# Last expert group of a fused transformer layer: down weights of the third expert ahead of the next gate and up weights, last down product in four column pieces, last scatter by token halves

## What is computed

```
for e in range(N_EXPERTS):                       # 32
    hid = silu(ht @ w_gate[e]) * (ht @ w_up[e])  # 2048 -> 512, twice
    out = out + gates[:, e:e + 1] * (hid @ w_down[e])   # 512 -> 2048
...
x = x + g2 * out
return rmsnorm(x, final_g)
```

## Time and profile before

| | us |
|---|---|
| median of 3 runs | 1431.66 (1430.23 to 1432.35) |
| the profiled execution | 1430.98 |
| its span, first to last instruction | 1429.1 |
| TensorE busy | 1311.6 (92%) |
| VectorE busy | 681.7 (48%) |
| ScalarE busy | 158.0 (11%) |
| GpSimd busy | 62.1 (4%) |

### The profile page before, as it was taken

The page is one execution under the profiler, slowest core; times in us unless marked ns, Lnnn a source line. Parts: engine busy times, 40 slices in busy tenths (PEclk is TensorE's granted clock), DMA queues, the critical chain, the costliest instruction groups (busy, mean ns, idle before and its releaser), DMA issues.

```text
span 1429.1 us, 14957 instructions
## 1 busy us (share of the span) xinstructions
PE 1311.6 (92%) x5797; PEld 663.2 (46%) x5797; DVE 681.7 (48%) x1069; ACT 158.0 (11%) x424; POOL 62.1 (4%) x74
## 2 busy tenths in 40 slices
PE   4999999999999999999997998989899799888896
PEld 4686688577888635333332332333233233223332
DVE  5678788699987621432332331333233232232235
ACT  3300000295001302000000000000000000000002
POOL 1000000013000100000000000000000000000000
PEclk9999999999999999999999999999999999999999
DMA  9999999983999999999999999999999999999995
GB/s 337 394 396 387 399 401 392 392 287 117 397 400 422 354 426 425 425 425 423 427 427 427 425 425 427 423 430 425 425 427 427 427 425 425 428 425 428 423 425 206
DMA packets 102961, 569.11 MB, mean 398 GB/s; under 512 B 5216, under 2 KB 19808, under 8 KB 70272
## 3 DMA queue, kind: packets, MB, share of 16 engines
q1 hardware_dynamic: 102384, 567.67, 97.5%
q0 software_dynamic: 528, 0.78, 0.4%
HBM read 566.27 MB, written 2.16 MB: 398 GB/s over the span
## 4 chain that ended last, share of the span: by engine, by line
PE 68%; DMA 26%; DVE 2%; ACT 2%; issue 1%; SPq 1%; DVEq 0%; ACTq 0%
DMA ring<-in_w_up 25%; PE PS L1731 22%; PE PS L1490 12%; PE PS L1695 8%; PE PS L1784 6%; PE PS L1596 6%; PE PS L1493 4%; PE PS L1568 2%; DMA ring<-in_w_ada 1%; PE PS L1678 1%; PE PS L1657 1%; PE PS L1716 1%; PE PS L1517 1%; PE PS L1431 0%; PE PS L1746 0%
## 5 line engine op out<-in xcount | busy, mean ns | idle before, releaser
L1731 PE MATMUL PS<-ring,gysq 128*64 128x512 f32 x960 | 222.7, 619 | 40.6 <-DMA ring<-in_w_up 40.6
L1731 PE MATMUL PS<-ring,W 128*64 128x512 f32 x1024 | 236.7, 620 | 21.4 <-DMA ring<-in_w_up 21.4
L939 DVE SCALAR_TENSOR_TENSOR W<-ring,sm,W 128x1024 f32<-128x1024 f32 (+1 forms) x195 | 234.4, 1202 | 21.7 <-DMA ring<-in_w_ada 5.7
L1784 PE MATMUL PS<-ring,W 128*64 128x512 f32 x992 | 219.7, 595 | 12.4 <-ACT W L864 12.4
L1267 DVE TENSOR_TENSOR r<-r,PS 128x512 f32<-128x512 f32 x120 | 82.5, 687 | 232.2 <-PE PS L1695 232.2
L1490 PE MATMUL PS<-r,ring 128*128 128x256 f32 x768 | 167.2, 379 | 0.7 <-DVE r L978 0.7
L1731 PEld LDWEIGHTS PS<-ring,gysq 128*64 128x64 f32 x960 | 79.3, 143 | 183.2 <-issue 183.2
L1490 PEld LDWEIGHTS PS<-r,ring 128*128 128x128 f32 x768 | 145.7, 190 | 22.9 <-issue 3.4
L1731 PEld LDWEIGHTS PS<-ring,W 128*64 128x64 f32 x1024 | 76.6, 142 | 170.2 <-issue 170.2
L1272 DVE TENSOR_SCALAR W<-W 128x256 f32<-128x256 f32 x32 | 21.0, 658 | 280.4 <-ACT W L860 279.6
L1784 PEld LDWEIGHTS PS<-ring,W 128*64 128x64 f32 x992 | 69.4, 137 | 142.3 <-issue 134.4
(11 more groups left out here) (273 smaller groups left out, 833.7 us busy)
## 6 DMA issues: line engine op xcount, KB each, us to landing
ring<-in_w_gate SPq DMA_DIRECT2D x64, 2048.0 KB, 25.5
ring<-in_w_up SPq DMA_DIRECT2D x64, 2048.0 KB, 28.0
ring<-in_w_down SPq DMA_DIRECT2D x64, 2048.0 KB, 28.4
ring<-in_w_ada SPq DMA_DIRECT2D x32, 2048.0 KB, 18.1
ring<-in_w_ada SPq DMA_DIRECT2D x32, 1024.0 KB, 16.2
ring<-in_w_qkv SPq DMA_DIRECT2D x9, 2048.0 KB, 19.0
ring<-in_w_o SPq DMA_DIRECT2D x8, 2048.0 KB, 17.6
ring<-in_w_qkv SPq DMA_DIRECT2D x8, 1536.0 KB, 16.9
```

The costliest lines, as they stand in the source:

```text
L939: ins = V.scalar_tensor_tensor(total, w, cT[:, t:t + 1], total, ALU.mult, ALU.add)
L1731: last = mm(PS[64 * j:64 * j + 64, i % 2, :].rearrange("p (m n) -> p m n", m=2), hE[i % 2][:, k], w[:, :, t, 256 * j:256 * j + 256], start ...
L1784: last = mm(PS[64 * q:64 * q + 64, bank + i2, :], hidT[:, b, 64 * j:64 * j + 64], w[:, b, 512 * ch:512 * ch + 512], start=(j + b == 0), st ...
```

## The change

The last group gets an order of its own, `LAST_GROUP`: gate and up 0 and 1, down 0 and 1, gate and up 2 and 3, down 2 and 3. TensorE does down 1 and the scatter of experts 0 and 1 ahead of gate and up 2; transpose 2 and six `keep_warm` matmuls stand between the halves of gate and up 3; transpose 3 stands between the halves of down 2, for which the last transposed hidden tile lies in a buffer of its own (`hidT_last`). The down weights of expert 31 come as four column pieces of 512, two to a ring slot, the first of each slot with a semaphore of its own (`piece_in`). Their products all go to PSUM partitions 64 to 127, of banks 0 to 3, and each piece has its own result on VectorE. The last scatter goes by token halves: four column chunks of tokens 0 to 127, then four of the rest; the first half's norm then needs four squares, and its root stands ahead of the last square on ScalarE. The window copy of GpSimd for the first expert of a group waits for 16 used chunks of the group before, where it waited for 14. ScalarE's loop over groups ends one turn earlier, with the last turn written out.

```diff
+LAST_GROUP = ([(0, k) for k in range(4)] + [(1, k) for k in range(4)] + [(0, 4), (0, 5), (1, 4), (1, 5)]
+              + [(2, k) for k in range(4)] + [(3, k) for k in range(4)] + [(2, 4), (2, 5), (3, 4), (3, 5)])
+LAST_GU_AT = [LAST_GROUP.index((i, 0)) for i in range(4)]
+LAST_DN_AT = [LAST_GROUP.index((i, 4)) for i in range(4)]
+TAIL = [(h, ch) for h in range(2) for ch in range(4)]
...
+            def last_down(ch, s):
+
+                n0 = D * (ch % 2)
+                return (slot(s)[:, n0:n0 + D].rearrange("p (t n) -> p t n", n=512), down_v[E - 1, :, :, 512 * ch:512 * ch + 512])
...
-                i, k = GROUP[m % 24]
+                i, k = (GROUP if m < EXP_CHUNKS * E - 24 else LAST_GROUP)[m % 24]
                 e = 4 * (m // 24) + i
                 if e == E - 1 and k >= 4:
-                    dst, src = last_down(k - 4, (S0 + m) % RING)
+                    dst, src = last_down(2 * (k - 4), (S0 + m) % RING)
+                    sp.dma_start(dst, src).then_inc(piece_in[k - 4], 16)
+                    dst, src = last_down(2 * (k - 4) + 1, (S0 + m) % RING)
...
-                    free = GU_END[i - 2] if i > 1 else GU_END[i + 2] - 24
+                    free = GU_END[i - 2] if i > 1 else max(GU_END[i + 2], LAST_GU_AT[i + 2] + 4) - 24
...
+                if tail:
+                    hidT_evac(1)
+                    exp_gate(2)
+                    selT_evac(2 * q + 1)
+                    hidT_evac(2)
+                    exp_gate(3)
+                    hidT_evac(3)
+                    return
...
-            with act.Fori(1, E // 4) as g:
+            with act.Fori(1, E // 4 - 1) as g:
                 expert_group(g)
+            expert_group(E // 4 - 1, tail=True)
...
-            last_root(0)
+                if k == 6:
+                    last_root(0)
             last_root(1)
...
+            def last_result(ch):
+
+                if ch % 2 == 0:
+                    dve.wait_ge(piece_ps, ch // 2 + 1)
+                else:
+                    dve.wait_ge(pe_chunk, PE0 + EXP_CHUNKS * E - 1 + ch // 2)
+                n0 = 512 * ch
+                V.tensor_tensor(yd[64:128, n0:n0 + 512], PS[64:128, ch, :], g2b[64:128, n0:n0 + 512],
+                                ALU.mult).then_inc(yd_ok, 1)
...
-                dve.wait_ge(f_ms, (6, 8)[h])
+                dve.wait_ge(f_ms, 4 * h + 4)
...
                 pe.wait_ge(hidT_ok, 4 * g + 4)
-                for j in range(2):
-                    w = slot(chunk_at(g, DN_AT[3] + j)).rearrange("p (b n) -> p b n", b=4)
-                    for b in range(4):
-                        for q in range(2):
-                            last = mm(PS[64 * q:64 * q + 64, j, :], hidT[:, b % 2, 64 * (b // 2):64 * (b // 2) + 64],
-                                      w[:, b, 512 * q:512 * q + 512], start=(b == 0), stop=(b == 3))
-                    last.then_inc(pe_chunk, 1)
                 p = 2 * g + 1
                 pe.wait_ge(selT_ok, p + 1)
+                for ch in range(4):
+                    if ch % 2 == 0:
+                        s = (S0 + LAST_DN_AT[3] + ch // 2) % RING
+                        pe.wait_ge(piece_in[ch // 2], 16)
+                    else:
+                        s = chunk_at(g, LAST_DN_AT[3] + ch // 2)
+                    w = slot(s)[:, D * (ch % 2):D * (ch % 2) + D].rearrange("p (b n) -> p b n", b=4)
+                    for b in range(4):
+                        last = mm(PS[64:128, ch, :], hidT_last[:, b % 2, 64 * (b // 2):64 * (b // 2) + 64], w[:, b],
+                                  start=(b == 0), stop=(b == 3))
+                    last.then_inc((piece_ps, pe_chunk)[ch % 2], 1)
                 for k, (h, ch) in enumerate(TAIL):
-                    if k % 4 == 0:
-                        pe.wait_ge(yd_ok, 4 * p + 4 + k // 2)
+                    if k < 4:
+                        pe.wait_ge(yd_ok, 4 * p + 3 + k)
...
+                if tail:
+                    hid_transpose(1)
+                    down(1)
+                    scatter(2 * g, more)
+                    gate_up(g, 2, tail=True)
+                    sel_transpose(2 * g + 1, 1)
+
+                    def third_transpose():
+                        hid_transpose(2)
+                        keep_warm(4, 6)
+
+                    gate_up(g, 3, third_transpose, tail=True)
+                    down(2, lambda: hid_transpose(3))
+                    last_expert()
+                    return
```

More of the change, by code:

```diff
@@ L75 @@
 DN_END = [k + 2 for k in DN_AT]
-TAIL = [(0, 0), (0, 1), (1, 0), (1, 1), (0, 2), (0, 3), (1, 2), (1, 3)]
+LAST_GROUP = ([(0, k) for k in range(4)] + [(1, k) for k in range(4)] + [(0, 4), (0, 5), (1, 4), (1, 5)]
[3 more added lines that the diff above has]
+TAIL = [(h, ch) for h in range(2) for ch in range(4)]
 TAIL_BANK = [6, 7, 4, 5]
@@ L324, in layer_kernel @@
         hidT = W[:, 5120:5376].rearrange("p (b n) -> p b n", b=2)
+        hidT_last = idr[:, :].rearrange("p (b n) -> p b n", b=2)
         g2b = W[:, 5376:5376 + D]
@@ L392, in layer_kernel @@
         landed = [sem(f"landed{s}") for s in range(RING)]
+        piece_in, piece_ps = [sem(f"piece_in{i}") for i in range(2)], sem("piece_ps")
         upper_in, late_in = sem("upper_in"), sem("late_in")
@@ L852, in selT_evac, with expert_group @@
                 A.activation(selT, PS[:, 2, 0:T], ACT.Copy).then_inc(selT_ok, 1)
-            def expert_group(q, rest=False):
+            def expert_group(q, rest=False, tail=False):
                 def exp_gate(i):
-                    act.wait_ge(pe_chunk, PE0 + 24 * q + GU_END[i])
+                    act.wait_ge(pe_chunk, PE0 + 24 * q + (LAST_GU_AT[i] + 4 if tail else GU_END[i]))
                     if i:
@@ L863, in hidT_evac @@
                     act.wait_ge(hd_ps, 4 * q + i + 1)
-                    A.activation(hidT, PS[:, 3, 0:T].rearrange("p (b n) -> p b n", b=2), ACT.Copy).then_inc(hidT_ok, 1)
+                    A.activation(hidT_last if tail and i == 3 else hidT, PS[:, 3, 0:T].rearrange("p (b n) -> p b n", b=2),
+                                 ACT.Copy).then_inc(hidT_ok, 1)
                 exp_gate(0)
@@ L1280, in silu_up, with result @@
                 V.tensor_tensor(hid, ex, PS[:, i % 2, T:2 * T], ALU.mult).then_inc(hid_ok, 1)
-            def result(g, i):
-                dve.wait_ge(pe_chunk, PE0 + 24 * g + DN_END[i])
+            def result(g, i, tail=False):
+                dve.wait_ge(pe_chunk, PE0 + 24 * g + (LAST_DN_AT[i] + 2 if tail else DN_END[i]))
                 bank = 2 if i == 3 else 4
@@ L1321, in expert_group @@
                 result(q, 0)
-                silu_up(q, 2)
-                result(q, 1)
+                if not tail:
+                    silu_up(q, 2)
+                result(q, 1, tail)
                 acc_add(2 * q)
+                if tail:
+                    silu_up(q, 2)
                 silu_up(q, 3)
@@ L1329, in expert_group @@
                 if tail:
-                    last_result(0)
-                    last_result(1)
+                    for ch in range(4):
+                        last_result(ch)
                     for k in range(8):
@@ L1719, in first_gate_up, with gate_up @@
                     last.then_inc(pe_chunk, 2)
-            def gate_up(g, i, between=None):
+            def gate_up(g, i, between=None, tail=False):
+                at = (LAST_GU_AT if tail else GU_AT)[i]
                 pe.wait_ge(win_ok, 4 * g + i + 1)
                 for half in range(2):
-                    s = chunk_at(g, GU_AT[i] + 2 * half)
-                    chunk_at(g, GU_AT[i] + 2 * half + 1)
+                    s = chunk_at(g, at + 2 * half)
+                    chunk_at(g, at + 2 * half + 1)
                     w = ring[:, s * SLOT:(s + 2) * SLOT].rearrange("p (m t n) -> p m t n", m=2, n=FE)
@@ L1767, in hid_transpose, with down @@
                     last.then_inc(hd_ps, 1)
-                def down(i):
+                def down(i, between=None):
                     pe.wait_ge(hidT_ok, 4 * g + i + 1)
@@ L1778, in down @@
                     for j in range(2):
-                        w = slot(chunk_at(g, DN_AT[i] + j)).rearrange("p (b n) -> p b n", b=2)
+                        w = slot(chunk_at(g, (LAST_DN_AT if tail else DN_AT)[i] + j)).rearrange("p (b n) -> p b n", b=2)
                         for b in range(2):
@@ L1786, in down @@
                         last.then_inc(pe_chunk, 1)
+                        if j == 0 and between:
+                            between()
                 pe.wait_ge(sel_ok, 2 * n + 2)
@@ L1803, in first_scatter @@
                     scatter(2 * g, more)
[L1805 to L1809, removed]
+                gate_up(g, 3, first_scatter)
                 sel_transpose(2 * g + 1, 1)
@@ L1812, in expert_group @@
                 hid_transpose(3)
[L1813 to L1819, removed]
+                down(3)
+                if follow:
+                    gate_up(g + 1, 0)
+                scatter(2 * g + 1, more)
             first_gate_up()
```

7 lines of the change are left out of this document (removed).

## The result

The changed kernel takes 1438.04 us (median, 1436.87 to 1439.78), the kernel before, run beside it, 1430.24 (1428.41 to 1434.96). The ratio is 1.0050, 95% interval 1.0036 to 1.0064: slower by some 7 us.

The account below looks back on a forecast made before the run. The weight stream bounds the earlier groups, TensorE's program order the last 73 us, VectorE the last 10. Last scatter +6.9 us later, root -0.5, sum +6.4 on the 1431.66 median: 1438.1 us, range 1434.5 to 1441.0.

Parts of the forecast that it names:

- D3: Last group's down product of expert 3 on TensorE: 13.8 us instead of 7.02, all on one output half.
- the warming: Six warming matmuls between the halves of expert 3's gate and up product: 2.6 us, covering no wait, paid in full.
- D0 to the end of D1, G2 and first scatter: Last group: down products of experts 0 and 1, expert 2's gate and up product, first scatter; 2.3 us gained.
- not lengthened: Rival: matmuls on one output half still overlap, D3 stays at 7.02 us, total 1431.3 or 1429.7; chance 0.08.
- open weight loads: Rival: each of D3's 32 weight loads adds its 0.14 us, 4.5 us more, total 1442.6; chance 0.05.
- Gap ahead of D1: TensorE idle before expert 1's down product, waiting for VectorE's result of expert 0: some 1.7 us, start at 1347.3.
- The clock: Low clock in first scatter, 9.11 us (lower bound 7.54); upper bound: expert 1's down product also slow, 1.57 us more.
- H3 inside D2: Expert 3's hidden transpose between the halves of expert 2's down product: input ready just in time at 1400.7, first half 3.51.
- Root and tail: Kernel end: first root ahead of the eighth square on ScalarE, 0.5 us sooner, and all that follows with it.
- Landings: Last group's weight chunks land every 4.89 us, the last (number 23) at 1404.3; no transfer waited for.
- SyncE: Transfer issue queue: nothing starves, the final gain is issued two us earlier, no cost.
- The new order: Last group's reordered TensorE list: 2.3 us gained by the end of expert 2's gate and up product.

Follow-up runs that it names:

- e1: Changed kernel with the last down product writing output partitions 0 to 63 and 64 to 127 in turn again; 1430.53 us, ratio 0.9995.
- e2: Kernel before with the last down product writing only output partitions 64 to 127, old order kept; 1437.69 us, ratio 1.0048.
- e3: Changed kernel without the six warming matmuls; 1435.22 us, ratio 1.0025.
- e4: Changed kernel with the last down product on both output halves and no warming matmuls; 1429.16 us, ratio 0.9987.
- e6: e1 with the last down weights loaded as two column halves of 1024 instead of four pieces; 1431.31 us, ratio 0.9997.
- e5: e4 with the last group's down product of expert 1 writing banks 6 and 7; 1429.48 us, ratio 0.9989.
- e9: e5 with the last down weights loaded as two column halves of 1024 instead of four pieces; 1428.43 us, ratio 0.9983.
- e8: Changed kernel with five warming matmuls in the idle ahead of the last group's down product of expert 1; 1435.37 us, one run.

## Why the prediction was right, point by point

- **The whole.** Forecast 1438.1 (1434.5 to 1441.0), measured 1438.04; forecast +6.4 us, measured +7.2 by the ratio (5.1 to 9.2) and +6.9 in the profiled pair. Part of the closeness is luck: before came out 1.4 us lower beside the changed kernel (1430.24) than in the three runs on which I built, and the medians moved 7.8 us where I had 6.4; the two errors cancel. In the profiled pair the +6.9 is made up of D3 +6.8, the warming +2.7, everything from D0 to the end of D1, G2 and first scatter -2.1, the tail -0.4, and some -0.1 for the transposes that moved.
- **D3, the deciding term.** Forecast 13.8, measured 13.82, and e1 and e2 take it out and put it in by itself: -6.9 and +6.9 us. The ground that I gave, the scatter's pitch as the price of a column stream, was an analogy when I wrote it; e2 shows it for the half alone. The rival "not lengthened" is ruled out, and so are open weight loads: the load of 0.14 us is followed by 0.29 of idle, inside the matmul's 0.43. The spacing of 0.216 us that the prediction worked out from the Trainium skill (TensorE: Matmul & The Clock Gate, section "Wait — 56ns, not 53.3ns?") is half of the 0.43 measured here in float32 at granted clock 1.00.
- **Gap ahead of D1.** The start was right (9.68 us behind D0's start forecast, 9.71 measured). I wrote "some 1.7 us" of idle; it is 2.25, and my own numbers gave 2.2 (1344.7 and 0.37 of H1 to 1347.3). The sum used the start, so nothing came of it but the clock.
- **The clock.** I put the low clock on the scatter and took D1's as the upper bound. It fell on D1 (8.79) and spared the scatter (7.60): +1.70 and -1.51, which nearly cancel: that the sum came out at its middle is luck too. e3, e4 and e6, the same program up to there, show both slow, e1 the same as here. So the forecast's middle was one of several outcomes, and three of these five executions lay nearer its upper part; that may be one reason why the medians moved more than 6.4, but only one execution of each kernel has a profile.
- **Warming.** Forecast 2.6 us paid in full, measured 2.68 (1387.42 to 1390.10), and 2.8 in the medians of e3.
- **H3 inside D2.** Forecast just in time; D2a to H3 took 3.68 us rather than 3.51, as its `hid` was ready at 1400.65.
- **Root and tail.** Forecast -0.5, measured -0.4.
- **Landings.** This is the step that was wrong, without harm to the sum. I took 4.89 us a chunk to the end and had chunk 23 at 1404.3, 97.8 us behind the block of the seventh group that waits for its weights:

```profile
1306.48 8.56 PE L1731 MATMUL PS<-ring,gysq 128*64 128x512 f32 x32 [2.69 <-DMA ring<-in_w_up]
```

  The changed kernel, e4, e5 and e9 all show 99.2 to 99.3: in e9 the last four chunks take 5.16 us each (1387.65 to 1408.30, 20.65 us for four). The 4.89 came from gate and up chunks, which pass at 428 GB/s (the kernel before, 1355 to 1380); the down chunks come last and pass more slowly, expert 2's at 418 (e5, 1390 to 1394), expert 3's at 384 to 410. In the changed kernel the last piece landed at 1406.7, and the fourth quarter of D3 began near 1414.9 (three quarters of 13.82 us behind 1404.56), so 8 us of slack hid the error. In e4, where D3 is short, the slack is gone, and the error made me expect 1.5 to 3.5 us of e5 that didn't come.
- **SyncE.** Wrong in size and sign: I had the final gain issued two us earlier; it was issued at 1395.33, 6 us later than before (1389.43 then), since one of the pieces held the queue for 9.23 us and the next for 3.72. With two halves in their place (e6) it went out at 1387.98, as forecast. Long issues are not the pieces' alone, though: in the kernel before one of the issues lasted 10.7 us. What the queue waited for no view shows. It cost nothing, as the gain is read 30 us later.
- **The new order.** Forecast: it wins 2.3 us and pays them to the warming. Measured 2.1 (from D0 to the end of D1, G2 and scatter 44.68 us before, 42.60 after), with one of the two blocks at the low clock. With both low, in e4, it is 0.7 (44.01). Without D3's loss and the warming e4 is faster than before by 0.6 to 3.1 us; the new tail's 0.4 is part of that. More the weight stream doesn't allow, as e5 and e9 show.

## What to carry to other kernels

When a matmul fills only half of the array's columns, look at which output partitions its neighbours in the program write: two in turn on both halves cost as much as one in this float32 kernel, and a rewrite that puts all on one half, for a tidier result or finer pieces, doubles the block. The weight loads show it at a glance: two in one pitch, or one. And before a reordering is judged by the waits it removes, write the new list with the landings beside it: an edit that fills an idle where there is none (the warming matmuls), or that makes an engine early for a transfer that is last (e5), shows itself on paper.

## What the runs showed of the hardware

- A 64-wide float32 matmul instruction of 512 columns on one half of the output partitions takes 0.43 us (the changed kernel and e2), as a 128-wide one does (L1758); two in turn on different halves share this time (e1, 6.97 us for 32).
- Behind an idle of 2.25 to 2.7 us the granted clock sometimes falls to the 1.2 GHz level for a while and sometimes doesn't, for programs that are the same up to there: the first scatter took 7.6 us in the changed kernel and e1, and 9.0 to 9.2 in e3, e4 and e6; behind a D1 at the full clock it took 7.6 in e9 and 9.1 in e5. Each fall cost 1.4 to 1.8 us. Behind the filled gap of e8, and behind one of 0.47 us in e5 and e9, it did not fall.
- The last down weights in runs of 2 KB passed at 384 GB/s and in runs of 4 KB at 410 (e6; the kernel before has 408 in the same stretch), with all DMA engines busy in both. The Trainium skill, DMA: Bandwidth & Descriptors, section Specifications, puts the least transfer for line rate at 512 B; this trace shows a 6% difference well above that.
